# SSD heads taken in pairs, with two banks for z, y of two heads on alternating column halves, and the sample states' rank one updates on GpSimd

## What is computed

```python
a = jnp.cumsum(dtc * A[:, None], -1)
decay = jnp.exp(jnp.where(causal, a[..., :, None] - a[..., None, :], -jnp.inf))
scores = jnp.einsum('bhtn,bhsn->bhts', cc, bc) * decay * dtc[..., None, :]
y = jnp.einsum('bhts,bhsp->bhtp', scores, xc) + jnp.exp(a)[..., None] * jnp.einsum('bhtn,bhpn->bhtp', cc, S0)
w = jnp.exp(aL[..., None] - a) * dtc
S1 = jnp.exp(aL)[..., None, None] * S0 + jnp.einsum('bhsp,bhsn->bhpn', xc * w[..., None], bc)
```

## Time and profile before

| | |
|---|---|
| median of 3 runs | 852.43 us (852.32 to 853.04) |
| the profiled execution | 855.75 us, its span 853.9 us, granted clock 0.984 |
| TensorE busy | 798.9 us (94%) |
| VectorE, ScalarE, GpSimd busy | 285.5, 209.4 and 29.2 us |
| the chain that ended last | TensorE 68%, DMA 24%, VectorE 4%, ScalarE 2% |
| DMA | 264.16 MB, 309 GB/s over the span |

### The profile page before, as it was taken

How to read it: one execution, slowest core, us unless ns; L and a number is a source line. 1 busy time by engine, 2 the same in 40 slices (tenths; PEclk the granted TensorE clock), 3 DMA queues, 4 the chain that set the end, 5 groups by cost and what they waited for, 6 DMA issues and landing times.

```text
span 853.9 us, 10128 instructions
## 1 busy us (share of the span) xinstructions
PE 798.9 (94%) x3825; PEld 428.0 (50%) x3825; DVE 285.5 (33%) x712; ACT 209.4 (25%) x585; POOL 29.2 (3%) x84
## 2 busy tenths in 40 slices
PE   7999999986899999999999899889999799999896
PEld 5877777764666778764322533223533235332232
DVE  4936437556787640151002102020030021021204
ACT  4246557533645300250100000000100000101013
POOL 7000000000000010000000000000000000000000
PEclk9999999998999999999999999999999999999999
DMA  9933636652567648335999999999999999999993
GB/s 261 320 139 91 221 114 210 220 197 68 185 184 230 209 205 365 129 123 228 428 428 427 427 427 427 427 428 429 428 427 429 426 428 427 428 428 427 427 412 141
DMA packets 75207, 264.16 MB, mean 309 GB/s; under 512 B 7270, under 2 KB 46442, under 8 KB 62856
## 3 DMA queue, kind: packets, MB, share of 16 engines
q1 hardware_dynamic: 73264, 259.02, 77.1%
q0 software_dynamic: 1680, 4.43, 1.5%
q10 hardware_dynamic: 216, 0.07, 0.1%
HBM read 251.68 MB, written 11.99 MB: 309 GB/s over the span
## 4 chain that ended last, share of the span: by engine, by line
PE 68%; DMA 24%; DVE 4%; ACT 2%; issue 1%; POOL 1%; SPq 0%; ACTq 0%; DVEq 0%; POOLq 0%
DMA ring<-in_w_up 20%; PE bank L2062 16%; PE bank L1681 12%; PE bank L1929 7%; PE bank L2124 6%; PE bank L2040 5%; PE bank L1669 4%; DMA ring<-in_w_down 3%; PE bank L2084 2%; PE bank L1760 2%; PE bank L1922 1%; PE bank L1628 1%; PE bank L1748 1%; PE bank L1821 1%; DVE h_tok L1270 1%
## 5 line engine op out<-in xcount | busy, mean ns | idle before, releaser
L2062 PE MATMUL bank<-ring,arena 128*64 128x512 f32 x1024 | 230.6, 596 | 19.2 <-DMA ring<-in_w_up 14.8
L2062 PEld LDWEIGHTS bank<-ring,arena 128*64 128x64 f32 x1024 | 69.9, 137 | 162.7 <-issue 134.4
L1681 PE MATMUL bank<-arena,ring 128*128 128x280 f32 x448 | 118.8, 420 | 9.4 <-DVE arena L1421 8.5
L2124 PE MATMUL bank<-ring,arena 128*64 128x512 f32 x480 | 106.6, 594 | 8.6 <-DMA ring<-in_w_down 8.6
L1681 PEld LDWEIGHTS bank<-arena,ring 128*128 128x128 f32 x448 | 86.6, 198 | 34.2 <-DVE arena L1421 9.0
L458 DVE COPY arena<-bank 64x512 f32<-64x512 f32 x15 | 10.3, 684 | 219.7 <-PE bank L2124 219.7
L2124 PEld LDWEIGHTS bank<-ring,arena 128*64 128x64 f32 x480 | 34.0, 137 | 78.8 <-issue 64.4
L1561 DVE TENSOR_TENSOR arena<-bank,arena 128x512 f32<-128x512 f32 x16 | 16.8, 1052 | 136.2 <-PE bank L2062 136.2
L1929 PE MATMUL bank<-arena,ring 128*128 128x264 f32 x256 | 58.7, 388 | 0.0
L1929 PEld LDWEIGHTS bank<-arena,ring 128*128 128x128 f32 x256 | 48.1, 190 | 9.4 <-issue 1.5
L1078 ACT ACTIVATE arena<-bank 128x512 f32<-128x512 f32 x16 | 9.6, 597 | 171.9 <-PE bank L2073 171.9
(11 more groups left out here) (357 smaller groups left out, 741.6 us busy)
## 6 DMA issues: line engine op xcount, KB each, us to landing
ring<-in_w_gate SPq DMA_DIRECT2D x32, 2048.0 KB, 18.5
ring<-in_w_up SPq DMA_DIRECT2D x32, 2048.0 KB, 23.2
ring<-in_w_down SPq DMA_DIRECT2D x30, 2048.0 KB, 21.7
ring<-in_w_in SPq DMA_DIRECT2D x9, 2048.0 KB, 9.8
out<-h_tok SPq DMA_DIRECT2D x16, 512.0 KB, 5.2
ring<-in_w_out SPq DMA_DIRECT2D x4, 2048.0 KB, 10.7
h_tok<-in_state_mlstm_C SPq DMA_DIRECT2D x8, 512.0 KB, 6.6
arena<-v_dram SPq DMA_DIRECT2D x8, 512.0 KB, 4.0
```

Source lines behind the costliest of these rows:

```text
L1681: last = mm(bank[5][:, 0:T], slot_k(UNIT_SLOT[u], 512)[:, k, o:o + P], hT[:, k, :], start=(k == 0), stop=(k == KD - 1))
L2062: last = mm(b[CAP * half:CAP * (half + 1), :], XG[:, k, e * CAP:(e + 1) * CAP], w[:, kk, half * 512:(half + 1) * 512], start=(k == 0), sto ...
L2124: last = mm(bank[5][CAP * half:CAP * (half + 1), :], HT[:, kk, u * CAP:(u + 1) * CAP], w[:, kk, half * 512:(half + 1) * 512], start=(u == ...
```

## The change

One turn of each SSD loop is now a pair of heads.

- TensorE makes z tiles into two banks in turn (`z_bank`: 4 and 5, later 5 and 1), so that a tile waits for the one two before it. Tile 1 and the first products of B and C (`decay_products(0)`) stand ahead of the transposes; the second products stand at pair 3, in bank 4.
- y of both heads is written block by block, the two heads' halves of the bank in turn.
- GpSimd does `s_update`: for each half of a sample's state a product into a buffer (`outer`) and an addition, both 128 x 512, each waiting for the one before.
- VectorE does `pair_weighted`, `s_read(c)` of the same pair (not of the pair before), `ssd_args` of the next two heads, then `ssd_out` and `gate_y` of the same pair.
- ScalarE does the last mLSTM head's evacuation ahead of `decay_state(HA)`, and the first two z tanhs ahead of its waits for the DMAs.

```diff
--- before.py
+++ after.py
+        def z_bank(n):
+            return bank[(4, 5)[n % 2] if n < KD else (5, 1)[n % 2]]
...
+            outer = carve(ring, tmp0 + 7174, 4, P)
+            def s_update(b):
+                pool.wait_ge(bb_in[b % 2], 16 * (b // 2 + 1))
+                pool.wait_ge(s.st_dec, HA + b + 1)
+                pool.wait_ge(s.st_new, HA + b)
+                for j in range(NG):
+                    part = state_buf(HA + b)[:, 4 * j:4 * j + 4, :]
+                    link(g.tensor_tensor(out=outer, in0=BB[:, b % 2, j * P:(j + 1) * P].unsqueeze(1).to_broadcast([P, 4, P]),
+                                         in1=XDS[:, 4 * j:4 * j + 4, b:b + 1].to_broadcast([P, 4, P]), op=ALU.mult))
+                    last = g.tensor_tensor(out=part, in0=part, in1=outer, op=ALU.add)
+                    if j == 0:
+                        link(last)
+                last.then_inc(s.st_new, 1)
             pool.wait_ge(s.n1_sb, 1)
             pool.dma_start(p_n[0, 0], NSTo[:, :]).then_inc(s.out_mn, 16)
             pool.dma_start(s_n[0].rearrange("b h d -> (b h) d"), N1T[:, :]).then_inc(s.out_mn, 16)
+            for b in range(5):
+                s_update(b)
             for half in range(2):
+                if half == 1:
+                    for b in range(5, NB):
+                        s_update(b)
                 pool.wait_ge(s.sst_ready, half + 1)
                 dst = p_S[0, 0].rearrange("h q n -> (h q) n").rearrange("(c p) n -> p c n", p=P)
                 pool.dma_start(dst[:, 4 * half:4 * half + 4, :],
...
-                tanh_of_conv(3 + 2 * h)
-                decay_state(h + 1)
-                evac(HA + XBC_A[h])
                 if h == HA - 1:
+                    evac(HA + XBC_A[h])
+                    tanh_of_conv(17)
                     first_tap(19)
+                    cq_copy(h)
                     tanh_of_conv(18)
+                    head_out(h)
                     tanh_of_conv(19)
-                cq_copy(h)
-                head_out(h)
+                else:
+                    tanh_of_conv(3 + 2 * h)
+                    decay_state(h + 1)
+                    evac(HA + XBC_A[h])
+                    cq_copy(h)
+                    head_out(h)
...
+            z_tanh(0)
+            decay_exp(HA + 1)
+            z_tanh(1)
+            act.wait_ge(s.bcs_ps, 1)
+            a.activation(BCS, bank[2][0:NB, :], ACT.Copy).then_inc(s.bcs_ready, 1)
+            lct_copy(3, bank[0], s.lct_sb)
+            lct_copy(4, bank[1], s.lct_sb)
+            act.wait_ge(s.bt_ps, 1)
+            a.activation(BT[:, 0:2, :], bank[2][:, :].rearrange("p (a b) -> p a b", b=256), ACT.Copy)
+            a.activation(BT[0:16, 2, :], bank[0][0:16, 0:256], ACT.Copy).then_inc(s.bt_ready, 1)
+            decay_state(HA)
             act.wait_ge(s.xdt_ready, 3)
             act.wait_ge(s.out_conv, 16 * 6)
             act.wait_ge(s.rows_out, 32 + 16 * HA + 16)
+            for c in range(KD):
+                if c >= 1:
+                    decay_exp(HA + 2 * c)
+                    decay_exp(HA + 2 * c + 1)
+                if c == 4:
+                    state_out(0)
+                weighted_x(c)
+                if c >= 1:
+                    y_square(c - 1)
+                    z_tanh(2 * c)
+                if c + 1 < KD:
+                    decay_state(HA + c + 1)
+                if c >= 1:
+                    z_tanh(2 * c + 1)
+                if c == 1:
                     a.preload_act_table(ACT.Sqrt)
                     act.wait_ge(s.rden_ready, 1)
                     a.activation(SCL[0:HA, :], SCL[0:HA, :], ACT.Sqrt, bias=epst[0:HA, 0:1], scale=1.0 / DH).then_inc(s.sc_exp, 1)
                     a.preload_act_table(ACT.Exp)
...
+            pair_weighted(0)
+            z_out(0)
+            z_out(1)
...
+            denominators()
+            for c in range(KD):
+                if c >= 1:
+                    pair_weighted(c)
+                if 1 <= c < 4:
+                    z_out(2 * c)
+                if c >= 4:
+                    num_out(c - 4)
+                s_read(c)
+                if 1 <= c < 4:
+                    z_out(2 * c + 1)
+                if c + 1 < KD:
+                    ssd_args(2 * c + 2)
+                    ssd_args(2 * c + 3)
+                ssd_out(dve, c)
+                gate_y(c)
+                if c == 0:
+                    head_squares()
+                if c == 2:
                     head_scales()
...
-                b5_tile(U_Z + n // 4, (n % 4) * P, B5_Z + n)
+                if n == KD + 1:
+                    pe.wait_ge(s.sst_ready, 1)
+                earlier = n if n == KD else max(n - 1, 0)
+                b5_tile(U_Z + n // 4, (n % 4) * P, B5_Z + earlier, z_bank(n))
...
             z_tile(0)
+            pe.wait_ge(s.conv_done, NCONV)
+            decay_products(0)
+            z_tile(1)
             pe.wait_ge(s.xdt_ready, 3)
...
+            pe.wait_ge(s.bcs_ready, 1)
             pe.wait_ge(s.lct_sb, 3)
+            for j, (t0, m) in enumerate(S_TILES):
+                for g_ in range(NG):
+                    last = tr(bank[2 if j < 2 else 0][0:m, (j % 2) * 256 + g_ * P:(j % 2) * 256 + (g_ + 1) * P],
+                              CBX[:, KD + g_, t0:t0 + m], ident[:, :])
+            last.then_inc(s.bt_ps, 1)
...
+            for c in range(KD):
+                if c == 0:
...
+                    pe.wait_ge(s.n1_sb, 1)
+                else:
+                    z_tile(2 * c)
+                    if c >= 4:
+                        head_rows(c - 4)
+                    z_tile(2 * c + 1)
+                if c == 1:
+                    pe.wait_ge(s.bt_ready, 1)
+                    pe.wait_ge(s.lct_sb, 4)
+                    states(0)
+                if c == 3:
+                    pe.wait_ge(s.b5_free, B5_Z + 7)
+                    decay_products(1)
+                if c >= 1:
+                    states(c)
+                    group_sum(c - 1)
+                if c >= 2:
                     pe.wait_ge(y_free, c - 1)
-                q0 = HD * (h % 2)
                 for j, (t0, m) in enumerate(S_TILES):
-                    last = mm(yb[q0:q0 + HD, t0:NP], XDT[0:m, j, h * HD:(h + 1) * HD], ARG[0:m, h % 2, BLK[j]:BLK[j] + NP - t0],
-                              start=(j == 0), stop=(j == 2))
-                last.then_inc(s.y_ps, 1)
+                    for q in range(2):
+                        h, q0 = 2 * c + q, HD * q
+                        pe.wait_ge(s.st_done, HA + h + 1)
+                        last = mm(yb[q0:q0 + HD, t0:NP], XDT[0:m, j, h * HD:(h + 1) * HD], ARG[0:m, q, BLK[j]:BLK[j] + NP - t0],
+                                  start=(j == 0), stop=(j == 2), skip_group_check=True)
+                        if j == 2:
+                            last.then_inc(s.y_ps, 1)
```

More of the change, by code:

```diff
@@ L986, in _ @@
             act.wait_ge(s.rows_out, 32 + 16 * HA + 16)
-            for h in range(HB):
-                if h + 1 < HB:
-                    decay_exp(HA + h + 1)
-                if h % 2 == 0:
-                    weighted_x(h // 2)
-                elif h + 1 < HB:
-                    decay_state(HA + h // 2 + 1)
-                z_tanh(h)
-                if h % 2 == 0 and h >= 2:
-                    y_square(h // 2 - 1)
-                if h == 3:
+            for c in range(KD):
[13 more added lines that the diff above has]
+                if c == 1:
                     a.preload_act_table(ACT.Sqrt)
@@ L1400, in gate_y @@
                 v.tensor_tensor(YB[:, c, 0:NP], YB[:, c, 0:NP], ZB[:, c, 0:NP], ALU.mult).then_inc(s.yz_ready, 1)
-            sample_num()
-            for h in range(HB):
-                c = h // 2
-                dve.wait_ge(s.gt_ps, h // (HB // NG) + 1)
-                weighted(HA + h, bank[3 + h // (HB // NG)])
-                if h + 1 < HB:
-                    ssd_args(h + 1)
-                if h == 1:
-                    denominators()
-                if h == 4:
-                    head_scales()
-                if h % 2 == 0 and h >= 2:
-                    ssd_out(dve, c - 1)
-                    gate_y(c - 1)
-                    s_read(c - 1)
-                if h % 2 == 1:
-                    s_update(c)
-                if h < KD:
-                    dve.wait_ge(s.z_sig, h + 1)
-                    v.scalar_tensor_tensor(out=ZB[:, h, :], in0=ZB[:, h, :], scalar=1.0, in1=bank[5][:, 0:T],
-                                           op0=ALU.add, op1=ALU.mult).then_inc(s.b5_free, 1)
-                if h % 2 == 1 and h >= 9:
-                    num_out((h - 9) // 2)
@@ L1425, in _, with pair_weighted, z_out @@
-            ssd_out(dve, KD - 1)
-            gate_y(KD - 1)
-            s_read(NB - 1)
+            def pair_weighted(c):
+                dve.wait_ge(s.gt_ps, c // 4 + 1)
+                for h in (2 * c, 2 * c + 1):
+                    weighted(HA + h, bank[3 + c // 4])
+            def z_out(h):
+                dve.wait_ge(s.z_sig, h + 1)
```

(24 more changed lines are left out.)

58 lines of the change are left out of this document (12 added, 46 removed).

## The result

The changed kernel takes 839.25 us in the median of 4 runs (837.78 to 839.93), the kernel before 852.73 in the runs beside it; the ratio of the times is 0.9831, 95% interval 0.9804 to 0.9859. Measured again with more runs, it took 837.31 us against 854.48 (17 runs of before, 851.66 to 857.17), ratio 0.9799 (0.9773 to 0.9824). So the change is worth 2.0%, 17 us, inside the range that was given.

A forecast was written before the change was run, and what follows sets the result against it. The SSD stage, waiting on TensorE, was to pass its gain one for one to the DMA-bound expert loop: 10.9 us up to z tile 4 plus 7.8 after, less 1.6, is 17.1, giving 835.3 by the median; range 829.5 to 844.

The forecast's parts named there:

- Up to z tile 4: SSD stage's first part, through the samples' chain: z tile 4 at 210.5 instead of 221.38, a gain of 10.9 us.
- The wait ahead of the states of pair 1: TensorE, done with pair 0's states at 202, waits 3.6 us for ScalarE's `weighted_x(1)` at the end of the samples' chain.
- the slowing of VectorE: Rival, chance 0.10: GpSimd's update of sample 1 slows VectorE's reading and exponents; chain ends 3 to 4 us later, about 839.
- The low clock: TensorE's clock falls after the wait ahead of pair 1's states; 2.3 us charged ahead of z tile 4.
- From z tile 4 on: Pairs 2 to 7 of the SSD stage take 67.6 us in place of 75.35, a gain of 7.8 us.
- The 1.6 taken off for hand-overs: Deduction from the 18.7 us sum for small hand-overs not foreseen that may open in place of the old waits.
- No overlap of y: Rival, chance 0.13: alternating column halves don't run beside each other; seven pairs lose 0.92 us each, 6.4 in all, 841.7.
- GpSimd as the bound: Rival, chance 0.06: updates above 11.3 us set the pairs' pace; 867 us at 3.7 us an instruction.
- the prediction's slack: In a steady pair GpSimd's update has nine us before it is read; a slower update costs pair 1 alone.
- nothing is passed on: Rival, chance 0.04: something that doesn't move limits the experts' weights, so the earlier stage end is waited away; 851 to 853.
- the row-based 0.97: Time in us of one GpSimd update instruction, taken as two passes from other operations' rows; 4.0 an update with semaphores.

The follow-up runs named there:

- the run with y in turn: The changed kernel with y of one head written whole before y of the other, so column halves no longer alternate: 847.69 us, 10.4 more than the changed kernel.
- three reorderings: Sample 1's update held back, 839.83 us; pair 1's exponents and products ahead of sample 0's reading, 838.05; that order with updates on VectorE, 832.21 against its base's 832.07.

## Why the prediction was right

**Time and sign.** 835.3 was forecast; 839.25 was measured first, 837.3 with more runs, all in the range of 829.5 to 844. The gain of the stage was put at 17.1 us and is 16.7 between the first two profiles, 19.5 between the second two; by the medians of more runs the change is worth 17.2. Taking it from the median as it stands was 2 us off, since that median of three runs lay low. That the sum comes within half a microsecond is luck: its parts are off by up to 3.7 us, in both directions.

**Up to z tile 4** the steps hold to within half a microsecond as far as GpSimd's start in the first profile: z tile 0 at 178.80 (179.0 forecast; the two other profiles of this kernel have 177.02 and 177.22), tile 1 done at 187.5 (188.0), the update at 194.46 (194.6). Then two terms were mis-sized. The wait ahead of the states of pair 1, put at 3.6 us, is 6.54: the update took 4.52 instead of 4.0, and the slowing of VectorE, which I had as a rival at 0.10, is there in each profile: reading and exponents 2.3 us longer than alone. TensorE was also there 0.7 us sooner than forecast, behind states of pair 0 that ended near 201.3, not 202. The low clock, charged at 2.3, cost 3.9: states, sum and y took 2.2 longer and the two z tiles 1.6 (9.45 against 7.81). The gain up to there is 7.2 us, where 10.9 was forecast: z tile 4 at 212.58, and 1.6 for the clock, against 221.38.

**From z tile 4 on** it was 9.5, not 7.8: 65.8 us without the clock's share against 67.6, since y is 1.08 instead of 1.2, two z tiles take 7.65 to 7.85 instead of the 7.94 that the sum took (its own rows give 3.97 + 3.88), and a pair with its broadcast row thus 11.09 instead of 11.30. The 1.6 taken off for hand-overs thus covered errors of other places, and the sum is better than its parts.

**The rivals.** No overlap of y is refuted by the run with y in turn, which also prices it: y is worth at least the 8.2 us in its rows. GpSimd as the bound is refuted: doubled, it still leaves the late pairs at 11.09. Its price was set too low, though: 4.5 us more an update cost 12.7, where the prediction's slack left 4.5 to the first chain. That nothing is passed on is refuted by the weights' first load and the unchanged expert loop. That GpSimd slows VectorE was no rival but part of what happens, and it hid a question that I didn't ask: what the move of the updates is worth by itself. I costed it at nothing but its chain. It is worth minus 4.5 us (runs on two chips) to minus 5.1 (on one): with all the other parts and the updates left on VectorE the kernel takes 832 to 833.

**GpSimd's rate, and what it does to VectorE.** The Trainium skill, GPSIMD Engine Reference, section 3.1, gives a rate that would be 1.12 us an instruction, as an estimate; the rows have 1.05 and 1.09, so trace and page agree, and the row-based 0.97 was low. The Trainium skill, GPSIMD Engine Reference, section 8, says that contention comes with two inputs in SBUF. The trace agrees and adds the size: six exponents 1.75 us alone, 2.6 to 4.8 where GpSimd works beside them; `weighted`, with a bank as input, 0.57 in either case, as the run with GpSimd's work doubled shows.

The 4.6 us of the chain divide into 2.3 for the longer update and 2.3 for the slowing by rows; the run with sample 1's update held back bears this out for pair 1 alone, where the wait fell by 2.25 us. No run took the slowing out of all pairs and left the rest. A kernel that gives GpSimd only such times when VectorE reads banks wasn't tried.

## What to carry to other kernels

Before an elementwise operation moves from VectorE to GpSimd, list what VectorE does meanwhile: where that reads two inputs from SBUF, it pays back part of what it was spared (8.9 of 17.4 us here), and where the operation is in a chain, the chain grows by the difference of the two engines and by the slowing. A second bank for a producer and alternating column halves each carry much of the gain: taken back alone they cost 13 us, in this order of the queues, and 10. When a wait is reordered away, look at the same engine one stage on before counting it: three reorderings here moved waits of 1.5 to 6 us and gained nothing that the times show.

## What was not expected of the hardware

Eight of VectorE's 128x128 updates with a scalar took 2.19 us alone and 6.45 beside GpSimd; the 128x512 products 0.69 and 1.30 in the mean. GpSimd's own instructions grew less, from 1.05 to at most 2.6 us.

How long the slowed instructions take is not a multiple of their own time. In the nine profiles with GpSimd at work, 136 of VectorE's exponents, reading products and updates took over 1.25 times what they take alone, and each ended a fixed time behind the end of a GpSimd instruction: 0.55 us for 512 columns, 0.30 for 272, 0.16 for 144, 0.02 for 16 and 0.15 for the updates of 128, all within 0.01 us. So these instructions wait until the GpSimd instruction under way has ended, which is why a block of 16 columns grew from 0.22 to 1.04 us in the mean of the run with GpSimd's work doubled, the most for its size. The lengths of GpSimd's instructions were not varied, so whether shorter ones would hurt less is not shown.

And y of two heads on alternating halves costs nearly what one head did, 1.14 us a row for 12 passes against 1.13 for 6 before. In the trace of the changed kernel each pass on one half starts 0.006 or 0.007 us behind its twin on the other, blocks of 16 columns included.
